# Index scores of a sparse attention spread over thirteen in-projection tiles, with top-k rounds between their sums

## The reference, cut to what matters

```
dots  = einsum('bqhd,bsd->bqhs', qi, ki) * IDX_DIM ** -0.5
score = einsum('bqh,bqhs->bqs', wi * IDX_HEADS ** -0.5, relu(dots))
score = where(kpos <= qpos, score, -inf)
_, idx = top_k(score, 256)          # per block of 128 queries
```

## Time and profile before

| what | before |
|---|---|
| median of runs | 3597.99 us |
| profiled execution | 3597.02 us |
| its span | 3595.3 us |
| TensorE matmul busy | 3460.8 us (96%) |
| DVE busy | 2039.3 us (57%) |
| GpSimd busy | 1545.4 us (43%) |
| ACT busy | 770.5 us (21%) |
| tiles 16 to 71 of the in-projection | about 1046.8 to 1757.8 us of the span |

### The profile page before, as it was taken

One profiled execution on the slowest core, in us unless ns is written; L12 is line 12 of the kernel. 1 busy time (PEld: TensorE's weight loads), 2 busy tenths in 40 slices (PEclk: granted clock), 3 DMA queues, 4 the chain that ended last, 5 costly groups with the idle time before them and its releaser, 6 DMA issues.

```text
span 3595.3 us, 57385 instructions
## 1 busy us (share of the span) xinstructions
PE 3460.8 (96%) x22646; PEld 3266.6 (91%) x22646; DVE 2039.3 (57%) x3072; ACT 770.5 (21%) x1585; POOL 1545.4 (43%) x675
## 2 busy tenths in 40 slices
PE   8999999998999999999888889999999999999998
PEld 7999999998986999999767747879999999999998
DVE  5333333346666999987776644995283533324334
ACT  2000000012232111133576523762100200000000
POOL 3533443432322444444357513984444343453351
PEclk9999999999998999999799977999999999999999
DMA  2111111112211222232233236953351111111111
GB/s 91 53 47 35 53 53 35 46 47 78 56 31 47 89 95 90 84 97 90 60 100 89 80 86 159 244 145 96 107 175 51 40 55 35 42 57 41 41 54 57
DMA packets 392979, 272.33 MB, mean 76 GB/s; under 512 B 54970, under 2 KB 368650, under 8 KB 392856
## 3 DMA queue, kind: packets, MB, share of 16 engines
q1 hardware_dynamic: 373032, 225.76, 22.2%
q10 hardware_dynamic: 19824, 44.95, 3.3%
HBM read 211.05 MB, written 59.81 MB: 75 GB/s over the span
## 4 chain that ended last, share of the span: by engine, by line
PE 90%; DVE 4%; POOL 2%; issue 2%; ACT 2%; DMA 1%; ACTq 0%; DVEq 0%; SPq 0%; POOLq 0%
PE setA L365 10%; PE setA L366 10%; PE setB L365 10%; PE setA L367 10%; PE setB L366 10%; PE setB L367 10%; PE bankC L365 2%; PE bankC L367 2%; PE bankC L366 2%; PE bankD L367 2%; PE bankD L365 2%; PE bankD L366 2%; PE setB L517 1%; PE bankC L1498 1%; PE bankD L2118 1%
## 5 line engine op out<-in xcount | busy, mean ns | idle before, releaser
L345 POOL TENSOR_TENSOR whi<-wraw,ones 128x1024 fp32r<-128x1024 f32 x190 | 471.8, 2483 | 1634.3 <-PE setA L367 1044.2
L365 PE MATMUL setA<-hhi,whi 128*128 128x352 f32 (+1 forms) x2304 | 752.6, 327 | 20.8 <-POOL wlo L348 10.0
L365 PE MATMUL setB<-hhi,whi 128*128 128x352 f32 (+1 forms) x2304 | 747.9, 325 | 1.9 <-POOL wlo L348 1.9
L366 PE MATMUL setA<-hlo,whi 128*128 128x352 f32 (+1 forms) x2304 | 746.8, 324 | 0.0
L367 PE MATMUL setA<-hhi,wlo 128*128 128x352 f32 (+1 forms) x2304 | 745.8, 324 | 0.0
L366 PE MATMUL setB<-hlo,whi 128*128 128x352 f32 (+1 forms) x2304 | 743.0, 322 | 0.0
L367 PE MATMUL setB<-hhi,wlo 128*128 128x352 f32 (+1 forms) x2304 | 741.7, 322 | 0.0
L348 POOL TENSOR_TENSOR wlo<-wraw,whi 128x1024 fp32r<-128x1024 f32 x190 | 475.8, 2504 | 14.9
L365 PEld LDWEIGHTS setA<-hhi,whi 128*128 128x128 f32 x2304 | 437.2, 190 | 27.8 <-issue 18.5
L365 PEld LDWEIGHTS setB<-hhi,whi 128*128 128x128 f32 x2304 | 434.0, 188 | 6.3 <-POOL wlo L348 2.5
L366 PEld LDWEIGHTS setA<-hlo,whi 128*128 128x128 f32 x2304 | 437.0, 190 | 1.7
(11 more groups left out here) (423 smaller groups left out, 5716.2 us busy)
## 6 DMA issues: line engine op xcount, KB each, us to landing
wraw<-in_w_in SPq DMA_DIRECT2D x64, 512.0 KB, 3.7
wraw<-in_w_ffn_gate SPq DMA_DIRECT2D x44, 512.0 KB, 3.8
wraw<-in_w_ffn_up SPq DMA_DIRECT2D x44, 512.0 KB, 3.8
wraw<-in_w_ffn_down SPq DMA_DIRECT2D x44, 512.0 KB, 3.6
abc<-acsD SPq DMA_DIRECT2D x8, 2048.0 KB, 10.9
xcD<-cv ACTq DMA_DIRECT2D x24, 520.0 KB, 2.7
zD<-spill ACTq DMA_DIRECT2D x16, 524.0 KB, 2.7
sraw<-sD SPq DMA_DIRECT2D x2, 4192.0 KB, 13.1
```

The source lines that it names most:

```text
L345: pool.tensor_tensor(dst_cols(slot, hi), dst_cols(slot), ones[:, :].unsqueeze(1).to_broadcast([P, KD, P]), ALU.mult).then_inc(w_hi, 1)
L365: pe.matmul(out, w1, r1, start=start, stop=False)
L366: pe.matmul(out, w1, r2, start=False, stop=False)
```

## The change

The units are ordered with the head innermost. They are spread four to a tile over tiles 16 to 28: two behind the first chunk, two behind the second, none behind the third. On DVE, after each sum, `rounds_beside` adds 1400 to a budget and does as many top-k rounds of finished query tiles as it pays for, a round costing the tile's width plus 300. A query tile counts as finished two units after its last one, and its first round waits for GpSimd's mask. Fourteen z tiles (`SPILL2`) go to `spill2`, written out in ACT's and TensorE's programs, and the loops begin behind them. GpSimd's splits are interleaved with the masks by a rule: ahead of a query tile's mask, all splits up to the second tile after the one that holds the tile's last unit. LATE is now tiles 5 to 8, whose rounds end one conv step after another, with the bias right behind the last round; EARLY is what the spread rounds left of tiles 2 to 4, with the biases behind.

```diff
-        IDX_UNITS = [(t, h, o) for t in range(2, NT) for h in range(4) for o in range(0, WID[t], 512)]
+        IDX_UNITS = [(t, h, o) for t in range(2, NT) for o in range(0, WID[t], 512) for h in range(4)]
         IDX_END = {t: sum(u[0] <= t for u in IDX_UNITS) for t in range(1, NT)}
-        IDX_SLOT = [(0, IDX_END[3])] + [(IDX_END[t - 1], IDX_END[t]) for t in range(4, NT)]
+        IDX_TILES = (16, 29)
+        IDX_SLOT = [(4 * j + a, 4 * j + b) for j in range(IDX_TILES[1] - IDX_TILES[0])
+                    for a, b in ((0, 2), (2, 4), (4, 4))]
+        SPILL2 = 14
...
+            def split(j):
+                split_tile(pool, TILE_IN + j, raw_count(TILE_IN + j), j % 2, (gemm_done[j % 2], 3 * (ORD_IN + j // 2)))
+            for j in (18, 19):
+                split(j)
...
+            nxt = 20
             for t in range(2, NT):
+                last = next(s for s, (_, e) in enumerate(IDX_SLOT) if e >= IDX_END[t])
+                while nxt <= 16 + last // 3 + 2:
+                    split(nxt)
+                    nxt += 1
                 pool.wait_ge(idx_acc, IDX_END[t])
...
-                if j >= 16:
+                if IDX_TILES[0] <= j < IDX_TILES[1]:
...
-            for j in range(2, 18):
+            for j in range(2, 16 + SPILL2):
                 gemm_tile(pe, TILE_IN + j, ORD_IN + j // 2, j % 2, between=functools.partial(beside, j))
...
-            for j in range(2):
+            for m in range(SPILL2):
+                i, j = m // 2, m % 2
+                if i:
+                    act.wait_ge(slot_out[j], 16 * i)
                 for c, (o, w) in enumerate(CH):
...
-                    index_relu(3 * j + c)
+                    if 3 * m + c < len(IDX_SLOT):
+                        index_relu(3 * m + c)
...
+            made, left, room = 0, {t: rounds for t in range(2, NT)}, 0
+
+            def rounds_beside(u):
+                nonlocal made, room
+                room += 1400
+                t = next(t for t in left if left[t])
+                while room >= WID[t] + 300:
+                    if u < IDX_END[t] + 2:
+                        room = 0
+                        return
+                    if left[t] == rounds:
+                        v.wait_ge(sc_masked, t - 1)
+                    made = rounds_of(t, 1, made)
+                    left[t] -= 1
+                    room -= WID[t] + 300
+                    t = next(t for t in left if left[t])
             for u, (t, h, o) in enumerate(IDX_UNITS):
...
+                rounds_beside(u)
...
                 if t == 3:
                     for j in range(2):
-                        v.wait_ge(slot_out[j], 16)
+                        v.wait_ge(slot_out[j], 16 * (SPILL2 // 2))
...
-            LATE = (NT - 4, NT - 3, NT - 2)
+            LATE = tuple(range(5, NT))
+            LAST_STEP = {t: CONV_STEPS - (LATE[-1] - t) for t in LATE}
-            n = 0
+            n = made
             for t in EARLY:
-                n = rounds_of(t, rounds, n)
+                n = rounds_of(t, left[t], n)
+            for t in EARLY:
                 bias_of(t)
             for t in LATE:
-                n = rounds_of(t, rounds - CONV_STEPS, n)
+                n = rounds_of(t, rounds - LAST_STEP[t], n)
...
             for i in range(CONV_STEPS + 1):
-                if i:
-                    for t in LATE:
+                for t in LATE:
+                    if 1 <= i <= LAST_STEP[t]:
                         n = rounds_of(t, 1, n)
+                        if i == LAST_STEP[t]:
+                            bias_of(t)
                 for j in range(2):
                     conv(2 * i + j)
-                    if i == CONV_STEPS and j == 0:
-                        for t in LATE:
-                            bias_of(t)
```

More of the change, by code:

```diff
@@ L734, in build @@
         NU = len(NORM_UNITS)
-        IDX_UNITS = [(t, h, o) for t in range(2, NT) for h in range(4) for o in range(0, WID[t], 512)]
+        IDX_UNITS = [(t, h, o) for t in range(2, NT) for o in range(0, WID[t], 512) for h in range(4)]
         IDX_END = {t: sum(u[0] <= t for u in IDX_UNITS) for t in range(1, NT)}
-        IDX_SLOT = [(0, IDX_END[3])] + [(IDX_END[t - 1], IDX_END[t]) for t in range(4, NT)]
+        IDX_TILES = (16, 29)
+        IDX_SLOT = [(4 * j + a, 4 * j + b) for j in range(IDX_TILES[1] - IDX_TILES[0])
+                    for a, b in ((0, 2), (2, 4), (4, 4))]
+        assert IDX_SLOT[-1][1] == len(IDX_UNITS)
+        SPILL2 = 14
         QROWS = [P] * (NT - 1) + [LAST]
@@ L840, in pool_in @@
                 split_tile(pool, TILE_IN + 16 + j, raw_count(TILE_IN + 16), j, (gemm_done[j], 3 * (ORD_IN + 8)))
-            for j in range(2):
-                split_tile(pool, TILE_IN + 18 + j, raw_count(TILE_IN + 18), j, (gemm_done[j], 3 * (ORD_IN + 9)))
+            def split(j):
+                split_tile(pool, TILE_IN + j, raw_count(TILE_IN + j), j % 2, (gemm_done[j % 2], 3 * (ORD_IN + j // 2)))
+            for j in (18, 19):
+                split(j)
             pool.wait_ge(kit_stored, 32)
@@ L856, in pool_in @@
                                    pattern=[[-1, w]], channel_multiplier=1).then_inc(sc_masked, 1)
-            pool_rest(pool, TILE_IN + 20, ORD_IN + 10, (N_IN - 20) // 2)
+            if nxt % 2:
+                split(nxt)
+                nxt += 1
+            pool_rest(pool, TILE_IN + nxt, ORD_IN + nxt // 2, (N_IN - nxt) // 2)
         def pool_rest(pool, n0, q0, pairs):
@@ L912, in beside @@
                     index_scores(3 * (j - 16) + c)
-            for j in range(2, 18):
+            for j in range(2, 16 + SPILL2):
                 gemm_tile(pe, TILE_IN + j, ORD_IN + j // 2, j % 2, between=functools.partial(beside, j))
-            with pe.Fori(0, (N_IN - 18) // 2) as i:
+            with pe.Fori(0, (N_IN - 16 - SPILL2) // 2) as i:
                 for j in range(2):
-                    gemm_tile(pe, i * 2 + (TILE_IN + 18 + j), i + (ORD_IN + 9), j)
+                    gemm_tile(pe, i * 2 + (TILE_IN + 16 + SPILL2 + j), i + (ORD_IN + 8 + SPILL2 // 2), j)
         def act_in(act):
@@ L985, in index_relu @@
                     act.activation(relu[0:qn, u % 2, 0:n], CD[u % 2][0:qn, 0:n], ACT.Relu).then_inc(idx_relu, 1)
-            for j in range(2):
+            for m in range(SPILL2):
+                i, j = m // 2, m % 2
+                if i:
+                    act.wait_ge(slot_out[j], 16 * i)
                 for c, (o, w) in enumerate(CH):
-                    act.wait_ge(gemm_done[j], 3 * (ORD_IN + 8) + c + 1)
+                    act.wait_ge(gemm_done[j], 3 * (ORD_IN + 8 + i) + c + 1)
                     act.activation(spill2[:, j, o:o + w], SETS[j][:, c, 0:w], ACT.Silu).then_inc(gemm_evac[j], 1)
-                    if j == 0 and c == 0:
+                    if m == 0 and c == 0:
                         head_root(NU - 1)
-                    index_relu(3 * j + c)
-                act.wait_ge(gemm_evac[j], 3 * (ORD_IN + 9))
-                act.dma_start(zD[j * P:(j + 1) * P, :], spill2[:, j, :]).then_inc(slot_out[j], 16)
+                    if 3 * m + c < len(IDX_SLOT):
+                        index_relu(3 * m + c)
+                act.wait_ge(gemm_evac[j], 3 * (ORD_IN + 9 + i))
+                act.dma_start(zD[m * P:(m + 1) * P, :], spill2[:, j, :]).then_inc(slot_out[j], 16)
             act.wait_ge(idx_acc, len(IDX_UNITS))
@@ L999, in act_in @@
             for dst, pairs, func, m0 in ((zD, 8, ACT.Silu, 0), (gaD, 4, ACT.Sigmoid, 8), (gsD, 4, ACT.Sigmoid, 12)):
-                with act.Fori(1 if m0 == 0 else 0, pairs) as i:
+                with act.Fori(SPILL2 // 2 if m0 == 0 else 0, pairs) as i:
                     spill_tile_pair(act, dst, func, i + (q + m0), i + m0, i)
@@ L1089, in dve_in @@
             v.wait_ge(tok_evac, NT + 2)
[L1090 to L1103, removed]
             rounds = TOPK // 8
@@ L1116, in rounds_of @@
                 return first + n
+            made, left, room = 0, {t: rounds for t in range(2, NT)}, 0
[13 more added lines that the diff above has]
+                    t = next(t for t in left if left[t])
+            for u, (t, h, o) in enumerate(IDX_UNITS):
+                qn, n = QROWS[t], min(512, WID[t] - o)
+                v.wait_ge(idx_relu, u + 1)
+                dst = sc[0:qn, SOFF[t] + o:SOFF[t] + o + n]
+                if h == 0:
+                    v.tensor_scalar(dst, relu[0:qn, u % 2, 0:n], wi9[0:qn, t, 0:1], None, ALU.mult).then_inc(idx_acc, 1)
+                else:
+                    v.wait_ge(idx_acc, u)
+                    v.scalar_tensor_tensor(dst, relu[0:qn, u % 2, 0:n], wi9[0:qn, t, h:h + 1], dst,
+                                           ALU.mult, ALU.add).then_inc(idx_acc, 1)
+                rounds_beside(u)
+            v.wait_ge(kit_stored, 32)
+            v.wait_ge(idx_acc, len(IDX_UNITS))
+            v.memset(xraw[:, :, 0:4], 0.0).then_inc(xraw_zero, 1)
             def bias_of(t):
```

## The result

| what | before | after |
|---|---|---|
| median of runs, side by side | 3597.3 us (4 runs) | 3562.95 us (4 runs, 3561.58 to 3564.59) |
| ratio, with its 95% interval | 1 | 0.9906 [0.9894, 0.9918] |
| span of the profiled execution | 3595.3 us | 3559.9 us |

What follows compares the result with a forecast made beforehand. TensorE was taken as the bound nearly everywhere, DVE nearly a second. The 67.6 us of units become 0.6 + 37.4 + 1.0 + 2.5 + 1.0 = 42.5, gaining 25.1: 3573 us, range 3567 to 3588.

Steps and rivals of the forecast that it cites:

- the term of 37.4 us: TensorE, tiles 16 to 28: matmul time of the 26 two-unit slots, 1.66 us per 512-column slot; bounds 25 and 46.
- pairs wholly side by side: Rival on TensorE's slots: 12 us less TensorE, DVE caps the gain at about 29 us, 3569; chance 0.07.
- DVE caps the gain at about 29 us: DVE's path to the convolution: conv 0 fits by only 2 to 6 us, so DVE limits the gain.
- DVE's spare time: DVE, tiles 20 to 28: 1.8 us a tile unusable or lost to GpSimd's port, moving readiness from 1472.6 to 1489.
- My bound of 41.6 us: Convolution: conv 0 may end 41.6 us after that start, since TensorE needs ACT's next evacuation at its fifth conv tile.
- The root's wait: TensorE, tile 16: unit 1 still waits 1.0 us for the root of the last norm unit.
- The hand-over: Tiles 18 and 19: late first mask delays DVE's sums, then ACT's relus and TensorE's units; 2.5 us, bounds 0 and 6.
- The clock: TensorE around tile 16's idle time: 1 us for a fall of the clock, bounds 0 and 3.6.
- No wait for a relu behind tile 18: Sign of being right: TensorE's relu waits only a few microseconds around tiles 18 to 20; waits in every tile mean wrong.
- 81 rounds done by tile 29: Sign of being right, on DVE: 80 top-k rounds done by tile 29.
- The slower rival: Tiles 16 to 28: GpSimd's splits hold DVE's sums, 4.8 us a tile; 3605 in full, chance 0.07; partial form 3585.
- The row at 1084.65: Earlier trace, DVE: two score instructions took 3.40 us together, ending just after GpSimd's; cited for the DVE-GpSimd exclusion rule.

Runs made afterwards that it cites:

- the run with late slots: Changed kernel with units behind each tile's second and third chunks and GpSimd's mask of query tile 2 before the split of tile 19: 3559.78 us.
- the old order: Changed kernel with the units in the earlier order, head outside and key chunk inside: 3574.47 us, 0.9939 of before.
- no rounds: Changed kernel without `rounds_beside(u)`, so all top-k rounds follow the last sum: 3676.67 us, 1.0221 of before.

## Why the prediction was off

**The step that failed: "Scaled to 512 columns I take 0.51 + 0.95 = 1.46, with entry and exit 1.66 us a slot", the term of 37.4 us.** It measured 27.5, in the run with late slots: a 512-column slot costs 1.26 us, a 384-column one 1.04. The reading of the earlier trace rows was the error. At 1053.50 and 1053.88 two units start 0.38 us apart, and I took this lag for the price of overlapping. It was the second unit's own wait, for the relu of the unit two before it, though the row names no wait. ACT's timeline of the kernel before has that relu:

```profile
1053.35 0.48 ACT L985 ACTIVATE relu<-bankC 128x384 f32<-128x384 f32 x1
```

It ends at 1053.83, and the unit starts 0.05 us later; the two units had not become ready together. A lag of the array would have been tested by asking what each of the two could not start before. The scaling was uneven besides: 0.38 was stretched by 512/384 to 0.51, but the 0.86 behind it to 0.95 where the same factor gives 1.15; stretched alike, the term would have been 40.6. Taken as a fixed price and scaled with the columns, the lag put 10 us on the term and left the true case, pairs wholly side by side, as a rival with a chance of 0.07.

The Trainium skill (TensorEngine Tiling (Array Packing), section Key Properties) says that tiles of the array run weight loads and matmuls in parallel. I wrote that the trace shows this only in part; the rows at 1170.90 and 1059.70, with starts 0.00 and 0.01 us apart, agree with it wholly.

**"DVE caps the gain at about 29 us"** failed too, and would have held the range up even with the right unit price. The rounds began at 1085.55 (forecast 1084.6) and the first convolution at 1476.51, 391 us later, where the 361 us of rounds and 27 of sums that I had counted make 388. The 16.4 us that I added for DVE's spare time, 1.8 us in each tile, were not there: with 512-column tiles of 14.0 us instead of 14.8, and sums of 971 ns instead of 752, DVE waits only 4.7 us in all of that time (3.8 for relus, 0.9 for a mask). The spare was a difference of two estimates, and it fell with the first of them. So the first convolution started 28.3 us after ACT's last evacuation before it (1448.20), with 5 us to spare against the 33.2 measured above. My bound of 41.6 us for the end of the first convolution, with 4 or 8 us for the convolution itself, is what the runs gave (37.6 + 4 and 33.2 + 8).

**The small terms.** The root's wait was 1.0 as forecast, and 0.9 more for the broken pair. The hand-over was put at 2.5 and cost 1.94, of which only 0.82 is a wait. The clock, put at 1, took 1.6 in tile 16, and here chance has a part: of six runs with the same 1.0 us wait, three show a fall behind it (this one, its repetition and the budget of 800) and three a clock of 1.00 (the old order, no rounds, the budget of 2200); why is open. About 0.4 us of tile 16 I can't assign. Together 0.6 + 27.5 + 1.9 + 1.94 + 1.6 + 0.4 = 33.94, against the 33.9 read from the stretches. The other 1.7 us of the span's fall lie outside the stage and were not followed up.

**What held.** No wait for a relu behind tile 18, a clock of 1.00 from there on, 81 rounds done by tile 29, no wait of TensorE in the convolution. The slower rival, DVE held by GpSimd's splits in every tile, did not come: sums were stretched, by 0.2 us in the mean at 512 columns, since most begin when no split runs. The Trainium skill (SBUF — State Buffer, section Who interferes with whom) lets a two-input DVE instruction and a GpSimd one that reads SBUF exclude each other; the trace agrees, a sum of 128 columns that met a split at 1108.18 took 1.79 us, and MAX8 and MATCH_REPLACE8, with one large input, kept 557 and 543 ns beside the earlier trace rows. The row at 1084.65, which the prediction names for this rule, is another case: it is a sum of head 0 (L1095), with one large input and a column of head weights. It was held as well, to 0.15 us behind the split's end. The price is small here only because so little of DVE's time is sums.

## What to carry to other kernels

Two fp32 matmuls with a contraction of 64 cost as much as one if they lie on opposite halves of the rows and can both start at once: put them in pairs, and see that what either waits for was done a chunk earlier. When an overlap in a trace looks incomplete, first ask what the second instruction was waiting for, and don't scale the lag. Filling an idle engine between the items of a handed-on chain can be underdone and overdone: at a budget of 800 or 2200 instead of 1400 the whole gain of 34 us was gone.

## What the runs showed of the hardware beyond this

- From its start to the next GEMM matmul a 512-column pair took 1.05 us (1170.90 to 1171.95), and so did a single unit that ran last in its slot (1089.41 to 1090.46): the second unit of a pair is free, to the hundredth of a microsecond.
- Waits of TensorE among dense matmuls cost about twice their length in the run with a budget of 2200: 24.9 us of waits made the stage 48.8 us longer, with the mean clock at 0.90 instead of 0.99.
- In the run with late slots, which has no waits in that stage, units spread two by two into the GEMM kept the clock at 1.00 throughout; packed into two tiles they had left it at 0.81.
